# Projections of 256 tokens: the input's high and low parts in one product of 512 columns, their halves summed on VectorE

## What is computed

```python
def _swiglu(h, w_in, w_out):
    g, u = jnp.split(h @ w_in, 2, axis=-1)
    return (jax.nn.silu(g) * u) @ w_out          # hidden width 2816

# retention
proj = x @ w_in
q, k, v, gate = jnp.split(proj, [RET_QK, 2 * RET_QK, 2 * RET_QK + RET_V], axis=-1)
...
return (jax.nn.silu(gate) * y) @ w_out
```

## Time and profile before

| what | value |
|---|---|
| runs shown | 2558.09, 2554.52, 2553.98 us, median 2554.52 us |
| profiled execution | 2558.02 us, span 2556.2 us |
| TensorE busy | 2499.7 us (98%), 17486 matmuls recorded |
| VectorE busy | 1482.3 us (58%) |
| ScalarE busy | 1039.3 us (41%) |
| granted TensorE clock | 0.992 of full |

### The profile page before, as it was taken

One profiled execution on the slowest core, in us unless ns is written; L12 is line 12 of the kernel. 1 busy time (PEld: TensorE's weight loads), 2 busy tenths in 40 slices (PEclk: granted clock), 3 DMA queues, 4 the chain that ended last, 5 costly groups with the idle time before them and its releaser, 6 DMA issues.

```text
span 2556.2 us, 40528 instructions
## 1 busy us (share of the span) xinstructions
PE 2499.7 (98%) x17486; PEld 2263.7 (89%) x17486; DVE 1482.3 (58%) x1987; ACT 1039.3 (41%) x1406; POOL 199.1 (8%) x192
## 2 busy tenths in 40 slices
PE   8999999989999999999999999999999999999998
PEld 6888888978888888888888889999999999988998
DVE  5666655756565557553364665565565554565655
ACT  4222324634212233222243554443754454555544
POOL 0000000211000010000010000020010020144001
PEclk9999999999999999999999999999999999999999
DMA  8455445125435454453262276564555566663562
GB/s 281 154 187 175 165 156 169 51 64 180 148 131 182 136 166 159 140 174 103 78 203 68 82 231 199 172 211 152 167 178 183 174 207 197 200 157 107 161 213 89
DMA packets 376081, 405.99 MB, mean 159 GB/s; under 512 B 7264, under 2 KB 352176, under 8 KB 375904
## 3 DMA queue, kind: packets, MB, share of 16 engines
q1 hardware_dynamic: 375904, 403.40, 49.1%
HBM read 402.25 MB, written 1.12 MB: 158 GB/s over the span
## 4 chain that ended last, share of the span: by engine, by line
PE 87%; DVE 4%; ACT 3%; issue 3%; DMA 1%; POOL 1%; SPq 0%; DVEq 0%; POOLq 0%; ACTq 0%
PE bank L98 87%; DVE w_lo L109 1%; ACT w_hi L105 1%; PE bank L101 1%; POOL acc L109 1%; DMA w_raw<-in_ffn_w_in 0%; SPq L135 0%; DVE tmp L117 0%; DVE at_e L117 0%; ACT x_hi L105 0%; ACT at_e L106 0%; DVE df_sc L126 0%; ACT df_e L106 0%; ACT at_pT L105 0%; DMA w_raw<-in_ada_w 0%
## 5 line engine op out<-in xcount | busy, mean ns | idle before, releaser
L109 DVE TENSOR_TENSOR w_lo<-w_raw,w_hi 128x2048 fp32r<-128x2048 f32 (+3 forms) x333 | 698.2, 2101 | 689.3 <-ACT w_hi L105 688.6
L98 PE MATMUL bank<-x_hi,w_hi 128*128 128x256 f32 (+1 forms) x3000 | 959.4, 320 | 7.7 <-DVE w_lo L109 4.2
L98 PE MATMUL bank<-x_hi,w_lo 128*128 128x256 f32 (+1 forms) x3000 | 949.7, 317 | 0.0
L98 PE MATMUL bank<-x_lo,w_hi 128*128 128x256 f32 (+1 forms) x3000 | 945.6, 317 | 0.0
L105 ACT ACTIVATE w_hi<-w_raw 128x2048 fp32r<-128x2048 f32 (+3 forms) x333 | 578.5, 1741 | 361.9 <-PE bank L98 199.4
L98 PEld LDWEIGHTS bank<-x_hi,w_hi 128*128 128x128 f32 x3000 | 572.5, 191 | 53.5 <-issue 15.1
L98 PEld LDWEIGHTS bank<-x_hi,w_lo 128*128 128x128 f32 x3000 | 572.5, 191 | 32.4
L98 PEld LDWEIGHTS bank<-x_lo,w_hi 128*128 128x128 f32 x3000 | 570.6, 191 | 32.4 <-issue 0.7
L98 PE MATMUL bank<-hid_hi,w_hi 128*128 128x512 f32 (+1 forms) x1056 | 346.9, 328 | 0.0
L98 PE MATMUL bank<-hid_lo,w_hi 128*128 128x512 f32 (+1 forms) x1056 | 345.3, 327 | 0.0
L98 PE MATMUL bank<-hid_hi,w_lo 128*128 128x512 f32 (+1 forms) x1056 | 345.3, 327 | 0.0
(11 more groups left out here) (281 smaller groups left out, 2352.2 us busy)
## 6 DMA issues: line engine op xcount, KB each, us to landing
w_raw<-in_ffn_w_in SPq DMA_DIRECT2D x88, 1024.0 KB, 6.3
w_raw<-in_ada_w SPq DMA_DIRECT2D x72, 1024.0 KB, 8.2
w_raw<-in_ffn_w_up SPq DMA_DIRECT2D x44, 1024.0 KB, 5.2
w_raw<-in_attn_w_in SPq DMA_DIRECT2D x36, 1024.0 KB, 5.4
w_raw<-in_ffn_w_out SPq DMA_DIRECT2D x32, 768.0 KB, 4.7
w_raw<-in_ret_w_in SPq DMA_DIRECT2D x24, 1024.0 KB, 5.3
w_raw<-in_ffn_w_out SPq DMA_DIRECT2D x32, 640.0 KB, 4.1
w_raw<-in_odd_w_in SPq DMA_DIRECT2D x12, 1024.0 KB, 5.4
```

The source lines that it names most:

```text
L98: return Issued(self.eng and self.eng.matmul(out, lhsT, rhs, start=start, stop=stop, skip_group_check=loose))
L109: return Issued(self.eng and self.eng.tensor_tensor(out, a, b, op))
```

## The change

`product_joined` takes the place of `product3` for most projections of 256 columns. The high and low parts of the moving operand now stand at a fixed distance in one tensor (`x2_hilo`, `hid_hilo`, `rt_hilo`, `w_hilo`), and one matmul of 512 columns multiplies the stationary high part by both: the first half of the bank gets the high, the second half the low one. A second matmul of 256 columns adds stationary low by moving high to the first half. The result is the sum of the bank's halves, which VectorE makes: `sum_parts`, a reduction of pairs from 512 PSUM values to 256.

Joined are: in b1, c0 and c1 both units of every step but j = 0, and the first three of four pairs of output tiles in each half; the value projections of the even and odd mixers and of retention; retention's gate; all but the first four query and four key tiles of the dilated attention; three of four output pairs of retention. In number 2252 triples.

Who reads the banks changes too:

- feed-forward: `summed` puts g's sum into `sg` on VectorE, and ScalarE's silu reads and writes `sg`; `added` puts u's sum into `tmp`, and a product of `tmp` and `sg` follows;
- retention's gate: VectorE sums into the gate's tile, ScalarE's silu works in place;
- query and key tiles: VectorE sums where ScalarE copied; value tiles: a sum where VectorE copied;
- output tiles: VectorE adds the two halves to the hidden state one after the other.

The core of the diff:

```diff
+    def sum_parts(self, out, a):
+        return Issued(self.eng and self.eng.tensor_reduce(out, a, AX, ALU.add))
...
+def product_joined(e, bank, a_hi, a_lo, b_both, start, stop):
+
+    wide, narrow = b_both.rearrange("p s (a b) -> p s b a", a=2), by_turns(b_both[:, 0, :])
+    if stop:
+        e.matmul(bank[:, 0:256], a_lo, narrow, False, False, loose=True)
+        return e.matmul(bank[:, 0:512], a_hi, wide, False, True, loose=True)
+    e.matmul(bank[:, 0:512], a_hi, wide, start, False, loose=True)
+    return e.matmul(bank[:, 0:256], a_lo, narrow, False, False, loose=True)
+
+
+def parts(bank):
+
+    return bank[:, 0:2 * T].rearrange("p (s b a) -> p a b s", s=2, a=2)
...
+def out_joined(n, c):
+
+    return n == T and c < KC // 2 - 1
...
     def silu(j, q):
+        if n == T and j:
+            e.wait_ge(k.vector, (f, "summed", j, q))
+            e.activation(k.sg[:, q, 0:T], k.sg[:, q, 0:T], ACT.Silu).then_inc(k.scalar, (f, "silu", j, q))
+            return
         e.wait_ge(k.product, in_name(f, j, 0, q))
...
+    def summed(j, q):
+        e.wait_ge(k.product, in_name(f, j, 0, q))
+        e.wait_ge(k.vector, (f, "gated", j - 2, q))
+        e.sum_parts(halves(k.sg[:, q, 0:T]), parts(k.out_of(in_name(f, j, 0, q)))).then_inc(k.vector, (f, "summed", j, q))
...
+        if n == T and j:
+            e.sum_parts(halves(k.tmp[:, q, 0:T]), parts(k.out_of(in_name(f, j, 1, q)))).then_inc(k.vector, (f, "added", j, q))
+            e.wait_ge(k.scalar, (f, "silu", j, q))
+            e.wait_ge(k.vector, (f, "added", j, q))
+            e.tensor_tensor(k.tmp[:, q, 0:T], k.tmp[:, q, 0:T], k.sg[:, q, 0:T], ALU.mult).then_inc(k.vector, (f, "gated", j, q))
...
             dve_split(e, (f, "in", j, 0))
+            if n == T and j:
+                summed(j, 0)
+                summed(j, 1)
             if j:
                 dve_split(e, (f, "in", j, 1))
...
         for j in range(2):
-            e.wait_ge(k.product, ("ret_g", 2 * c + j))
-            e.activation(halves(t.gate[:, 2 * c + j, :]), in_order(k.out_of(("ret_g", 2 * c + j))[:, 0:T]), ACT.Silu).then_inc(
-                k.scalar, ("ret_g", 2 * c + j))
+            g = t.gate[:, 2 * c + j, :]
+            e.wait_ge(k.vector, ("ret_g_sum", 2 * c + j))
+            e.activation(g, g, ACT.Silu).then_inc(k.scalar, ("ret_g", 2 * c + j))
...
+        for m in (2 * c, 2 * c + 1):
+            e.wait_ge(k.product, ("ret_g", m))
+            e.sum_parts(halves(t.gate[:, m, :]), parts(k.out_of(("ret_g", m)))).then_inc(k.vector, ("ret_g_sum", m))
```

More of the change, by code:

```diff
@@ L161, with __init__ @@
 class Operand:
[L164 to L165 removed]
+    def __init__(self, tag, hi, lo, both=None):
+        self.tag, self.hi, self.lo, self.both = tag, hi, lo, both
 class Unit:
@@ L294, in wait_operand, with project @@
     e.wait_ge(e.k.vector, (x.tag, "lo", kk))
-def project(e, u, c, x, n, bank, ks=range(KC), k0=0, start=True, stop=True):
+def project(e, u, c, x, n, bank, ks=range(KC), k0=0, start=True, stop=True, joined=False):
     for kk in ks:
         wait_operand(e, x, kk)
+        if joined:
+            last = product_joined(e, bank, u.hi[:, kk - k0, c:c + P], u.lo[:, kk - k0, c:c + P], x.both[:, :, kk, 0:T],
+                                  start and kk == ks[0], stop and kk == ks[-1])
+            continue
         last = product3(e, bank[:, 0:n], u.hi[:, kk - k0, c:c + P], u.lo[:, kk - k0, c:c + P],
@@ L343, in pe_pair @@
         bank = e.bank(names[q], *taken[q])
-        project(e, u, q * P, x, n, bank).then_inc(e.k.product, names[q])
+        project(e, u, q * P, x, n, bank, joined=n == T and x.both is not None).then_inc(e.k.product, names[q])
     u.last = names[1]
@@ L788, in dve_gated @@
     e.wait_ge(k.vector, ("gate", stage))
+    if stage[0] == "b" and out_joined(n, kk // 2):
+        h, out = halves(k.hT[:, kk, 0:T]), [in_order(bank[:, i * T:(i + 1) * T]) for i in range(2)]
+        e.scalar_tensor_tensor(h, out[1], k.gate[:, kk, 0:1], h, ALU.mult, ALU.add).then_inc(k.vector, ("h_part", stage, half, kk))
+        e.wait_ge(k.vector, ("h_part", stage, half, kk))
+        e.scalar_tensor_tensor(h, out[0], k.gate[:, kk, 0:1], h, ALU.mult, ALU.add).then_inc(k.vector, ("h", stage, half, kk))
+        return
     for c in range(n // T):
@@ L812, in dve_residual @@
         ins = e.tensor_tensor(h, h, out, ALU.add)
+    if stage != "att_out" and out_joined(T, kk // 2):
+        ins.then_inc(k.vector, ("h_part", stage, half, kk))
+        e.wait_ge(k.vector, ("h_part", stage, half, kk))
+        ins = e.tensor_tensor(h, h, in_order(k.out_of(name)[:, T:2 * T]), ALU.add)
     ins.then_inc(k.vector, ("h", stage, half, kk))
@@ L837, in hidden @@
     at = MID if n == 2 * T else MID + FORTH
-    return Operand(tag, k.place("hid_hi", at, [P, 12, 2 * T], F32R), k.place("hid_lo", at + 24576, [P, 12, 2 * T], F32R))
+    both = k.place("hid_hilo", at, [P, 2, 12, 2 * T], F32R)
+    return Operand(tag, both[:, 0, :, :], both[:, 1, :, :], both)
 def in_name(f, j, base, q):
@@ L853, in pe_ffn @@
             names = [in_name(f, j, base, q) for base in range(2) for q in range(2)]
-            taken = [(k.scalar, (f, "silu", j, q)) for q in range(2)] + [(k.vector, (f, "gated", j, q)) for q in range(2)]
+            joined = n == T and j > 0
+            taken = ([(k.vector, (f, "summed", j, q)) if joined else (k.scalar, (f, "silu", j, q)) for q in range(2)]
+                     + [(k.vector, (f, "added" if joined else "gated", j, q)) for q in range(2)])
             if j == 0 and f == "a0":
@@ L928, in gated @@
         e.wait_ge(k.product, in_name(f, j, 1, q))
-        e.wait_ge(k.scalar, (f, "silu", j, q))
+        if not (n == T and j):
+            e.wait_ge(k.scalar, (f, "silu", j, q))
         if j == 0 and f in NORMED_BY:
@@ L2702, in dve_dilated, with out, summed @@
     t = Dilated(k)
-    over_tiles(e, ("att", 0), att_cols(0), dve_split, lambda i, name: None, lambda e: None)
+    def out(part):
+        def summed(i, name):
+            if i < 4:
+                return
+            e.wait_ge(k.product, name)
+            if part and i >= 10:
+                e.wait_ge(k.load("bias_rows"), ("bias_rows", 2))
+            e.sum_parts(halves((t.k if part else t.q)[:, i, :]), parts(k.out_of(name))).then_inc(
+                k.vector, ("att", part, i))
+        return summed
+    over_tiles(e, ("att", 0), att_cols(0), dve_split, out(0), lambda e: None)
     e.wait_ge(k.load("mask"), "mask")
```

66 lines of the change are left out of this document (40 added, 26 removed).

## The result

| | before | after |
|---|---|---|
| median of the runs compared | 2555.09 us (2553.98 to 2558.09, 4 runs) | 2618.14 us (2617.42 to 2621.59, 4 runs) |
| profiled execution | 2558.02 us | 2617.42 us |
| span | 2556.2 us | 2615.6 us |
| granted clock | 0.992 | 0.990 |

The ratio is 1.0244, 95% interval 1.0231 to 1.0257: slower by 63 us. The forecast was 2602 us, with 2566 to 2638 as the range. Between the profiled executions the loss is 59.4 us, where the sum on record gave 47.5.

The account below looks back on a forecast made before the run. TensorE's spacing of matmuls was taken to bound the kernel, as long as weights arrive. The terms -17 + 55 + 8.5 + 1 = +47.5 us gave 2602 us against a median of 2554.5, range 2566 to 2638.

Parts of the forecast that it names:

- the sum on record: Whole kernel: -17 (TensorE), +55 (feed-forwards), +8.5 (retention's gate), +1 (odd mixer), in all +47.5 us.
- TensorE's gain: 2252 joined triples: each takes 327.6 ns where it took 335.1, 7.5 ns less, 17 us saved in all.
- The reduction, 0.68: VectorE: each of 220 added reductions of 512 PSUM values to 256 was taken to cost 0.68 us.
- rival (b): Reductions cost 0.94 us each, 29 us more in the feed-forwards and 5 in the gate: 2636 us; chance 12%.
- rival (d): Reductions near 0.42 us, or more slack than counted: 30 us less, and 4 in the gate, 2568 us; chance 12%.
- The ring: Feed-forward steps: ScalarE and VectorE pieces, each waiting for the one before, take 13.3 us against TensorE's 10.5; chance 62%.
- Rival (a): The ring doesn't hold and the added VectorE work hides: 2538 us, faster; chance 9%.
- The feed-forwards: b1, c0, c1: TensorE 10.4 us late in the first half, 7.9 in the second, 18.3 each, +55 us.
- a clock under 0.95: Sign that the prediction is wrong: TensorE's clock below 0.95 inside the feed-forwards.
- rival (c): TensorE's clock falls in the ring's new gaps, 72 us more: 2674 us; chance 5%.
- The gate: Retention's gate: silu behind reductions behind w_lo makes TensorE 5.9 us late, last steps add 2 to 3: +8.5 us.
- all else: Other joined places: reductions covered by VectorE's idle time, except +1 us in the odd mixer.

Follow-up runs that it names:

- x16: x12 with retention's gate projected as before the change, without reductions: 2540.77 us, 0.9948 of before.
- x3: The changed kernel with only the g tiles of the feed-forward steps unjoined, u's reductions kept: 2554.08 us, 0.9988 of before.
- x9: The changed kernel with only the u tiles of the feed-forwards unjoined, g's reductions kept: 2572.04 us, 1.0057 of before.
- x5: The changed kernel, all joined, with both units of a feed-forward step rounded and split ahead of silus and sums: 2556.35 us, 0.9997 of before.
- x11: The changed kernel, all joined, with g's sums ahead of the w_lo of the step's first unit behind j = 2: 2551.69 us, 0.9985 of before.
- x4: The changed kernel with each g tile reduced twice, the second reduction waiting for the first: 2660.22 us, 1.0404 of before.
- x12: x11 with the sums of retention's gate also ahead of the next w_lo, all 2252 triples joined: 2544.43 us, 0.9956 of before.

## Why the prediction was right, point by point

**TensorE's gain: right.** Query and key tiles show it unstalled. ScalarE's roundings there, after; before they stood 5.36 us apart (2094.76 and 2100.12):

```profile
2149.43 1.92 ACT L105 ACTIVATE w_hilo<-w_raw 128x2048 fp32r<-128x2048 f32 x1 [3.32 <-PE bank L98]
2154.66 1.92 ACT L105 ACTIVATE w_hilo<-w_raw 128x2048 fp32r<-128x2048 f32 x1 [3.32 <-PE bank L98]
```

These two are 5.23 us apart and the next 5.25; 5.24 for 16 triples is 327.5 ns, 7.6 less than 335.1, where 7.5 was taken. x16 got 15 of 15.9 us from it. The Trainium skill (TensorE: Matmul & The Clock Gate, section Back-to-back issue gap) gives the spacing from which the prediction drew 2.5 ns a triple for an isolated matmul, and says that it doesn't hold for a stream of weight loads and matmuls, which the prediction left out. The rows here are such a stream, and their 7.6 ns decides.

**The reduction, 0.68: right** (0.683). That puts rival (b), 0.94, and rival (d), 0.42, out.

**The ring: right, and shown.** x3 against x9 (same count, other place), x5 and x11 (all reductions, other order) and x4 (one more each, 0.70 us each) can't be had from VectorE's load. Rival (a) is out too. In the times of c0, shifted by the 26.24 us by which the unit of the earlier trace rows starts later (1927.93), the steps' first roundings were to start at 1939.14, 1952.44, 1965.74 and 1979.04; they started at 1939.22, 1952.67, 1966.13 and 1979.58. The links that were short are the reduction to its product, 0.79 us (1949.13 to 1949.92) where 0.71 was taken, and silu to rounding, 0.32 us (1944.67 to 1944.99) where 0.28 was.

**The feed-forwards: mis-sized, +55 where it was about +65.** From its first silu to its last update of the hidden state, b1 takes 188.4 us where it took 169.5, and c0 188.3 where it took 169.5; c1, from its first silu to the kernel's end, takes 199.4 where it took 182.5. That is 54.6 us more, and TensorE's gain on their 1356 triples, 10.2 us, is already in it. Beside x12 TensorE ends the first half of each 11.1 us late (10.4 on record). When it goes on behind the last wait of the second half it is 19.9 us late, so that this half adds 8.8 (7.9 on record). The longer ring gives 0.6 and 0.5 of the difference. A third of 65 is 21.6 us for one feed-forward; the 1.7 us of it that are left come behind the last wait, and no run isolates them.

**TensorE's clock: hardly a part.** Windows of the kernel after (us, busy us of each engine, clock, DMA), around the last waits of b1 and then around those of c0:

```profile
1661.41:1665.41 4.00, 1.78 (x8) 1.20 (x8) 2.90 (x6) 1.29 (x3) 0.00 (x0) 1.00 0.52 164
1665.41:1669.41 4.00, 3.83 (x22) 3.33 (x23) 3.27 (x4) 1.88 (x2) 0.00 (x0) 1.00 0.14 22
...
2080.00:2084.00 4.00, 1.78 (x8) 1.20 (x8) 2.89 (x6) 1.29 (x3) 0.00 (x0) 0.96 0.51 164
2084.00:2088.00 4.00, 3.86 (x15) 3.44 (x16) 3.23 (x4) 3.35 (x4) 0.00 (x0) 0.61 0.10 16
```

The last two waits are the same in both to 0.01 us, 0.86 us and then 1.40 us. In c0 the clock fell behind them, to 0.61 in a window, most of it at the 1.2 GHz level; in b1 it stayed at 1.00, as in c1. TensorE goes on 19.9 us late in all three. Its last matmul of the feed-forward is 20.3 us late in b1 and c1 and 21.5 in c0, so the clock cost TensorE 1.2 us, once; at the last update of the hidden state b1 is 21.3 us late and c0 21.5. In c0's first half the clock fell too (0.67 in a window), and TensorE was 11.1 us late there as in b1, where it didn't. So the sign that I had named, a clock under 0.95, shows in single windows without the cost of rival (c). No run tried the clock by itself. The Trainium skill (TensorE: Matmul & The Clock Gate, section Why this matters for your kernels) warns of idle gaps between bursts; here the same waits left the clock at either level.

**The gate: the mechanism right, the size small.** In the retention stage everything starts 18.06 us later than before (1793.44 for 1775.38); the rounding of the earlier trace rows was to start 8.4 later than that, and did, at 1847.44. TensorE's timeline after:

```profile
1841.97 5.48 PE L98 MATMUL bank<-x_hilo,w_hilo 128*128 128x512 f32 x32 [0.89 <-DVE rt_g L129]
1851.76 7.05 PE L98 MATMUL bank<-x_hilo,w_hilo 128*128 128x512 f32 x32 [4.31 <-issue]
```

With 0.47 us before these two the waits are 5.7, where 5.9 was summed. The stage takes 230.2 us for 221.7: 8.4 net, where 5.9 was on record (8.5 less the gain of its 352 triples). The unit behind the long wait takes 7.05 us where the one before took 5.48; the clock in the 8 us from 1850 is 0.70 and 0.88. For the last steps 2 to 3 us had been added without working; TensorE waits 1.34 us there, and the rest is not found.

**The sum.** In the profiles the feed-forwards cost 9.8 us more than on record and the gate 2.5; all else gains 0.4 more. That is the 12 us between 47.5 and 59.4. The rest to 63 is that the profile before lay 2.9 us above the median compared, and the one after 0.7 below. The forecast of 2602 was 16 us low; the span that it gave the ring by itself, 2585 to 2620, holds 2618 near its upper end.

## What to carry to other kernels

When an operation moves from an engine that waited for TensorE to one that sits between two pieces of another's work, write down the links of one step around both in-order engines, start to start, and compare the sum with TensorE's step. Busy shares (62 and 39% here) don't show a ring. If it is longer, first move the small operation ahead of the long one that waits for the other engine: here that one move was worth 66 us of 2618 in the feed-forwards.

## What the hardware showed that was not expected

A reduction's time went by what it reads: 512 PSUM values to 256 took 0.683 us, 512 to one 0.685. And TensorE's clock, 1.00 in windows of steady work, fell to 0.61 behind waits of 0.86 and 1.40 us in one feed-forward and stayed at 1.00 behind the same waits in the two others. The waits alone don't say which of the two comes.
